# A pitch of 2080 and 2064 bytes in place of 2048 for the inner tiles of the feed-forward

## The reference

```
def _swiglu(x, w_gate, w_up, w_down):
    return (jax.nn.silu(x @ w_gate) * (x @ w_up)) @ w_down
...
h = h + 0.5 * _swiglu(_rmsnorm(h, ffn1_norm[l]), ffn1_w_gate[l], ffn1_w_up[l], ffn1_w_down[l])
h = h + _mixer(_rmsnorm(h, mix_norm[l]), w_in[l], ...)
h = h + 0.5 * _swiglu(_rmsnorm(h, ffn2_norm[l]), ffn2_w_gate[l], ffn2_w_up[l], ffn2_w_down[l])
return _rmsnorm(h, final_norm)
```

## Time and profile before

| | |
|---|---|
| median of three runs | 1799.57 us |
| profiled execution, first to last instruction | 1798.7 us |
| TensorE matmuls | 1786.7 us busy (99%), 10012 |
| TensorE weight loads | 1506.3 us (84%), 10012 |
| VectorE | 958.3 us (53%) |
| ScalarE | 632.9 us (35%) |
| GpSimd | 90.8 us (5%) |
| mean granted TensorE clock | 0.998 |

### The profile page before, as it was taken

One profiled execution on the slowest core, in us unless ns is written; L12 is line 12 of the kernel. 1 busy time (PEld: TensorE's weight loads), 2 busy tenths in 40 slices (PEclk: granted clock), 3 DMA queues, 4 the chain that ended last, 5 costly groups with the idle time before them and its releaser, 6 DMA issues.

```text
span 1798.7 us, 26473 instructions
## 1 busy us (share of the span) xinstructions
PE 1786.7 (99%) x10012; PEld 1506.3 (84%) x10012; DVE 958.3 (53%) x1385; ACT 632.9 (35%) x1002; POOL 90.8 (5%) x92
## 2 busy tenths in 40 slices
PE   9999999999999999999999999999999999999998
PEld 7888888888788888888988888888888888888887
DVE  5444443379888888622544446654334544444333
ACT  5322322244444454332333334443222323222221
POOL 2111100000000000000000000000000011111000
PEclk9999999999999999999999999999999999999999
DMA  5323223333233332223222222222222322223332
GB/s 171 105 93 100 98 94 105 106 99 90 83 82 93 87 86 84 82 95 103 94 71 71 93 82 93 90 84 73 102 95 94 103 90 99 93 94 103 106 105 72
DMA packets 53938, 169.30 MB, mean 94 GB/s; under 512 B 6337, under 2 KB 13761, under 8 KB 53873
## 3 DMA queue, kind: packets, MB, share of 16 engines
q1 hardware_dynamic: 45824, 159.15, 27.1%
q10 hardware_dynamic: 8048, 9.24, 2.6%
HBM read 166.21 MB, written 2.16 MB: 94 GB/s over the span
## 4 chain that ended last, share of the span: by engine, by line
PE 97%; DVE 2%; DMA 0%; ACT 0%; issue 0%; POOL 0%; SPq 0%; DVEq 0%; ACTq 0%; POOLq 0%
PE G L546 50%; PE I L546 16%; PE G L613 12%; PE G L566 8%; PE I L1040 1%; PE I L1016 1%; PE I L1006 1%; PE G L868 1%; PE I L673 1%; PE I L808 1%; PE I L817 1%; PE I L827 1%; PE I L794 0%; PE I L976 0%; PE I L980 0%; PE I L778 0%
## 5 line engine op out<-in xcount | busy, mean ns | idle before, releaser
L1657 DVE TENSOR_TENSOR WL<-RAW,WH 128x1024 fp32r<-128x1024 f32 x296 | 372.0, 1260 | 288.7 <-ACT WH L1137 279.4
L1137 ACT CAST WH<-RAW 128x1024 fp32r<-128x1024 f32 x295 | 307.1, 1046 | 223.3 <-PE I L546 126.4
L546 PE MATMUL G<-UH,WH 128*128 128x512 f32 x664 | 164.3, 389 | 0.0
L546 PE MATMUL G<-UL,WH 128*128 128x512 f32 x664 | 164.0, 389 | 0.0
L546 PE MATMUL G<-UH,WL 128*128 128x512 f32 x664 | 164.0, 389 | 0.0
L546 PEld LDWEIGHTS G<-UL,WH 128*128 128x128 f32 x664 | 124.6, 188 | 25.9
L546 PEld LDWEIGHTS G<-UH,WL 128*128 128x128 f32 x664 | 124.6, 188 | 25.9
L546 PEld LDWEIGHTS G<-UH,WH 128*128 128x128 f32 x664 | 124.5, 188 | 25.8
L546 PE MATMUL G<-NH,WH 128*128 128x512 f32 x448 | 114.8, 398 | 0.3 <-ACTq L1291 0.3
L546 PE MATMUL G<-NL,WH 128*128 128x512 f32 x448 | 110.7, 389 | 0.0
L546 PE MATMUL G<-NH,WL 128*128 128x512 f32 x448 | 110.7, 389 | 0.0
(11 more groups left out here) (351 smaller groups left out, 2622.3 us busy)
## 6 DMA issues: line engine op xcount, KB each, us to landing
RAW<-in_slabs SPq DMA_DIRECT2D x296, 512.0 KB, 3.4
cum_rows<-kept_rows ACTq DMA_DIRECT2D x16, 256.0 KB, 6.8
bias<-in_rel ACTq DMA_DIRECT2D x16, 128.0 KB, 2.8
bias<-in_rel ACTq DMA_DIRECT2D x16, 112.0 KB, 2.6
h<-in_x SPq DMA_DIRECT2D x6, 256.0 KB, 6.4
out_y<-h SPq DMA_DIRECT2D x4, 256.0 KB, 2.2
h<-in_x ACTq DMA_DIRECT2D x2, 256.0 KB, 3.5
out_y<-h ACTq DMA_DIRECT2D x4, 128.0 KB, 1.8
```

Source lines behind the costliest of these rows:

```text
L546: ins = mm(dst, slab(W, n)[:, (k - k0) * P:(k - k0 + 1) * P], R[:, k, :], start=begin and which == 0 and k == k0, stop=end and which == 2 ...
L1137: nc.scalar.copy(slab(WH, n), RAW[:, n.slot, :]).then_inc(split_hi, 1)
L1657: V.tensor_tensor(slab(WL, n), RAW[:, n.slot, :], slab(WH, n).bitcast(F32), ALU.subtract).then_inc(split_lo, 1)
```

## The change

Each of the two buffers gets a few unused elements behind every tile, so that tile k + 1 of `HH` begins 2080 bytes after tile k and tile k + 1 of `HL` 2064 bytes after tile k. The readers and writers name columns 0 to 511. The halves in `last_half` name their columns already.

```
+HH_STEP, HL_STEP = 8, 4
...
-        HH = sb("HH", [P, FT, T], F32R, r)
-        HL = sb("HL", [P, FT, T], F32R, r)
+        HH = sb("HH", [P, FT, T + HH_STEP], F32R, r)
+        HL = sb("HL", [P, FT, T + HL_STEP], F32R, r)
...
-                        ins = mm(dst, slab(W, n)[:, (k - k0) * P:(k - k0 + 1) * P], R[:, k, :],
+                        ins = mm(dst, slab(W, n)[:, (k - k0) * P:(k - k0 + 1) * P], R[:, k, 0:T],
...
-                    nc.scalar.copy(HH[:, bass.ds(ft, 1), :].rearrange("p a t -> p (a t)"),
+                    nc.scalar.copy(HH[:, bass.ds(ft, 1), 0:T].rearrange("p a t -> p (a t)"),
...
             def tile_of(ap, k):
-                return ap[:, bass.ds(k, 1), :].rearrange("p a t -> p (a t)")
+                return ap[:, bass.ds(k, 1), 0:T].rearrange("p a t -> p (a t)")
```

## The result

The changed kernel is slower. Its median is 1805.38 us (1803.54 to 1805.99) against 1799.56 us of the kernel before, run beside it; the ratio is 1.0029, with a 95% interval of 1.0017 to 1.0041. That is 5.8 us more, where I had forecast 4.4 less. The rival "the lock is lost" had given 1806.1. The time lies inside the range I had stated, 1790.5 to 1806.0 us, only because the upper part of that range stood for this rival.

The account below looks back on a forecast made before the run. TensorE's own matmul pace was taken as the bound. Register instructions and writes cost nothing, moving reads saved 2.5 us for HH and 1.9 for HL: 1799.57 - 4.4 = 1795.2 us, range 1790.5 to 1806.0 us.

Parts of the forecast that it names:

- the lock is lost: Rival, matmuls reading HH and HL: changing relation to the weights' reads costs 6.5 us at the middle, 1806.1 us; chance 0.24.
- What bounds the kernel: Whole kernel: only TensorE's own pace sets the time; each matmul reading HH or HL pays 13.33 ns over its columns.
- The register instructions and the writes: VectorE: 27 more register instructions, 2.2 us, hidden by slack; writes into HH and HL keep their shapes; both costed at nothing.
- The moving reads: Matmuls reading HH and HL: 3.33 ns less for each of 748, 5.0 less for each of 374, together -4.4 us.
- the grid: Moving reads: next tile starts on 64-byte steps counted from the last one's start; downwards -4.4 us, chance 0.33; upwards 0.04.
- its signs, scattered starts and longer matmuls: Down stages, if the lock is lost: starts scatter between 227 and 236 ns, matmul durations rise above 389 to some 395.
- Nothing: Rival, moving reads: the extra belongs to the exchange of weights, addresses don't matter at 512 columns, 1799.6 us; chance 0.20.
- The formula that I took from the Trainium skill: Matmul pace: warm gap N / 2.4 + 2.5 ns, 215.8 for 512 columns; at most 12.2 us to be had, 1787.4 us.

Follow-up runs that it names:

- The first experiment: Kernel before with HH and HL both beginning 32 bytes later, pitch 2048 as before: 1805.97 us, ratio 1.0046.
- The far pitch: Kernel before with a pitch of 2560 bytes for HH, 2048 for HL, both bases as before: ratio 0.9998.
- The shift of everything: Kernel before with 32 unused bytes behind h, so every later buffer, activations and weights alike, begins 32 bytes later: 1799.57 us, ratio 0.9999.
- The experiments with 32 and 64 bytes: Kernel before with HH and HL both 32, or both 64, bytes later against the weights, pitch 2048: ratios 1.0046 and 1.0012.

## Why the prediction was wrong

*What bounds the kernel* held. TensorE's pace was the only thing on the path, the 990 + 132 matmuls were the right ones to count, and all of the change lies in the two pieces of the chain that I had named. The gate-and-up and token-major pieces stayed as they were.

*The register instructions and the writes* were rightly put at nothing, though the new instructions took 40 ns each and not 80.

*The moving reads* are the term that failed, first in sign. I had costed them at 3.33 and 5.0 ns less per matmul, from the inference that a next tile starts on a grid of 64 bytes counted from the last one, so that a pitch of 2080 would need a smaller extra. The first experiment refutes the inference: with the pitch left at 2048 every tile starts on the grid counted from the last, and the pace rose to 233.3 ns all the same. (The far pitch doesn't decide here, since 2560 is a multiple of 64 too.) The shift of everything shows that a start off the 64-byte grid of addresses costs nothing either. The tile's relation to the stationary blocks is what matters, and for 512 columns zero, the one the kernel had, is with 256 the best of those tried. The measured term is 230.21 - 224.40 = +5.8 us for the 990, and about -0.1 us for the halves.

*How I went wrong* can be put on one row. I took the token-major stretch (117.8 ns) as a sign that less than 13.33 ns extra was within reach, and carried it over to matmuls of 512 columns. The experiments with 32 and 64 bytes show that the two widths answer differently: what makes 256 columns quicker (3.3 and 2.3 ns) makes 512 slower (6.7 and 2.2 ns). I had no row of 512 columns in another constant relation, and took the extra over the columns to be the same for both widths. At a relation of 32 it isn't: by the same price of a column it is 20.0 ns for 512 and 10.0 for 256.

*The rival "the lock is lost"* was right in place and in price, and in its signs, scattered starts and longer matmuls: I had 5.8 ns as the middle for each of 1122, and it was 5.9 for 990. Its reason was half right. I had thought the relation need only stay constant; a constant one of 32 or 128 bytes costs 6.7 ns, more than the changing one. What the change does, as far as the runs show, is to spend most tiles in relations other than zero, and to carry the disturbance over to the next ones when it passes zero. The evidence for it was in the earlier trace rows, and I gave it 0.24 where the grid, which rested on a pattern in three numbers, had 0.33.

*"Nothing"* came with a rule of the Trainium skill, "SBUF — State Buffer", section "Who interferes with whom": two independent read ports, and TensorE never waits. I drew from it that the change does nothing. The pace of one and the same stream went from 226.7 to 233.3 ns by a shift of its tiles of 32 bytes, and stayed at 226.7 when the weights were shifted too. The measurement decides: the pace does depend on how the moving tiles lie to the stationary blocks. Whether this happens at the read ports no run shows.

The formula that I took from the Trainium skill, "TensorE: Matmul & The Clock Gate", section "Back-to-back issue gap", stands there for an isolated matmul and not for a stream, as I had called it. Its 215.8 ns was reached in no run: the least for 512 columns was a pace of 226.7.

What stays open is what in the chip makes it so. That both sides of the relation are equivalent was shown; that it counts modulo 256 bytes rests on one pair. That the weight load's reads and the moving reads meet somewhere is the natural reading and wasn't tested by itself. All blocks lie 512 bytes apart, so the runs can't tell whether a matmul's own block counts or the next one, which is loaded beside it. Relations between those of the table, and steps under 32 bytes for a constant shift, weren't tried. Nor does the table explain the size of the 5.8 us: a pitch of 2112 passes through relations of 0, 64, 128 and 192 in about equal shares and costs 4.8 ns per matmul, and the table has 0, 2.2 and 6.7 for the first three. By an estimate from these, 192 alone would have to cost 10 ns, or moving from one relation to another costs something by itself, as the groups that pay behind a shifted one suggest.

## What to carry to other kernels

When a matmul stream is the bound, compute start-to-start times for each width from unbroken pieces of the chain, and note how moving tiles and stationary blocks lie to each other modulo 256 bytes: here a relation of 32 or 128 bytes cost 3% of a 512-column matmul. Padding the tiles of a moving operand changes that relation at every tile, so where 512 columns move and the relation is zero, don't pad, or pad so that it stays zero: 512 bytes per tile cost nothing here. That 256 would do follows from the reading modulo 256 and wasn't run as a pitch. For another width measure anew, since 256 columns were quickest at 32 bytes and not at zero.

## What the runs showed of the hardware that was not expected

A matmul of 512 columns on float32r with its weight load, with blocks 512 bytes apart and the granted clock at 1.00, has a pace of 226.7 ns at relations of 0 and 256 bytes, 228.9 at 64, and 233.3 at 32, 128 and 480. One of 256 columns has 120.0 ns at 0 and 256, and 116.7 at 32, 117.7 at 64, 118.7 at 128, 118.3 at 480. After a disturbance, the good pace comes back only after one to nine matmuls, so a disturbed group makes the next group pay: eight matmuls in the good relation took 230 ns each, on the mean, behind eight in a changing one. Writes by VectorE to tiles that begin off a 64-byte boundary took 693 ns, for 692 on it.
